# A two-layer transformer program put into one block, its stage barriers replaced by waits on data, and the end of its last expert layer rearranged

## The reference, cut to what matters

```
# first part
h = ada(rms_norm(x));  a = dsa_attention(h);  b = mla_attention(h)
x = x + (sigmoid(gd)*(a @ w_br_dsa) + sigmoid(gm)*(b @ w_br_mla)) @ w_out   # the mix
x = x + memory_cross_attention(rms_norm(x), mem)
x = x + moe(rms_norm(x))              # 16 experts in 4 groups, 2 taken, width 256
# second part, on ctx and x
[ctx, x] += gate * ssd_mixer(rms_norm([ctx, x]))
[ctx, x] += gate * expert_choice(rms_norm([ctx, x]))   # 16 experts of width 1024, each takes 32 rows of a stream
x += gate * attention(rms_norm([ctx, x]))
x += gate * expert_choice(rms_norm(x))
out = rms_norm(x) * final_norm_w
```

## Time and profile before

| | |
|---|---|
| median of three runs | 2198.77 us (2197.3, 2198.77, 2200.84) |
| the profiled execution: its time, its span | 2203.04 us, 2201.2 us |
| mean granted TensorE clock | 0.978 |
| PE, DVE, ACT, POOL busy | 2015.5 us (92%), 941.5 (43%), 648.8 (29%), 106.7 (5%) |
| read from device memory | 620.80 MB, mean 283 GB/s over the span |
| ends of the eight inner blocks | 101.2, 158.1, 213.3, 280.4, 354.1, 585.0, 1070.4, 1721.6 us |

### The profile page before, as it was taken

How to read it: one execution, slowest core, us unless ns; L and a number is a source line. 1 busy time by engine, 2 the same in 40 slices (tenths; PEclk the granted TensorE clock), 3 DMA queues, 4 the chain that set the end, 5 groups by cost and what they waited for, 6 DMA issues and landing times. The chain is left out here.

```text
span 2201.2 us, 24642 instructions
## 1 busy us (share of the span) xinstructions
PE 2015.5 (92%) x9980; PEld 1059.4 (48%) x9980; DVE 941.5 (43%) x1655; ACT 648.8 (29%) x1285; POOL 106.7 (5%) x121
## 2 busy tenths in 40 slices
PE   9987988999899999999899998988999899999887
PEld 6844444444377888878643333322445432222222
DVE  4776224444688878863612221212565310000002
ACT  5244023111277677662221111100235111111000
POOL 0101010000010110010100000000110000000000
PEclk9989998999899999999999999999999999999999
DMA  9537477899333433323589999999830599999996
GB/s 342 194 115 286 172 282 293 338 389 389 112 99 107 143 115 113 118 77 148 216 344 427 427 427 428 428 428 428 327 115 1 231 422 427 425 428 426 425 427 291
DMA packets 142768, 623.58 MB, mean 283 GB/s; under 512 B 10912, under 2 KB 61216, under 8 KB 104512
## 3 DMA queue, kind: packets, MB, share of 16 engines
q1 hardware_dynamic: 138144, 601.92, 68.6%
q0 software_dynamic: 2352, 16.91, 2.0%
q10 hardware_dynamic: 2160, 3.18, 0.4%
HBM read 620.80 MB, written 1.18 MB: 283 GB/s over the span
## 5 line engine op out<-in xcount | busy, mean ns | idle before, releaser
L2901 PE MATMUL bank<-slots,xgTe 128*64 128x512 f32 (+1 forms) x1664 | 373.4, 595 | 34.8 <-DMA slots<-in_moe_w 33.1
L3121 DVE TENSOR_TENSOR actse<-sge,bank 32x512 f32<-32x512 f32 (+1 forms) x48 | 32.8, 683 | 503.6 <-PE bank L2901 281.2
L2901 PEld LDWEIGHTS bank<-slots,xgTe 128*64 128x64 f32 (+1 forms) x1664 | 107.4, 124 | 276.8 <-issue 228.6
L2901 PE MATMUL bank<-slots,aTe 128*64 128x512 f32 (+1 forms) x704 | 161.8, 602 | 13.9 <-issue 13.9
L3019 ACT ACTIVATE sge<-bank 32x512 f32<-32x512 f32 (+1 forms) x48 | 28.4, 591 | 483.6 <-PE bank L2901 483.4
L529 PE MATMUL bank<-slots_r 128*128 128x512 f32 x416 | 164.1, 395 | 0.0
L528 PE MATMUL bank<-hT_r,slots_r 128*128 128x512 f32 x384 | 155.6, 405 | 0.0
L530 PE MATMUL bank<-slots_r 128*128 128x512 f32 x384 | 152.0, 396 | 0.0
L598 PE MATMUL bank<-slots,hT 128*128 128x512 f32 (+1 forms) x320 | 133.2, 578 | 5.3 <-DVE hT L495 3.0
L2125 DVE TENSOR_TENSOR slots_r<-slots,slots_r 128x2048 fp32r<-128x2048 f32 x32 | 76.7, 2397 | 68.2 <-ACT slots_r L2120 68.1
L372 POOL TENSOR_SCALAR rstd<-eps_rows 128x1 f32<-128x1 f32 (+5 forms) x41 | 17.5, 427 | 1768.0 <-ACT xn L445 619.2
(11 more groups left out here) (567 smaller groups left out, 3123.9 us busy)
## 6 DMA issues: line engine op xcount, KB each, us to landing
slots<-in_moe_w SPq DMA_DIRECT2D x148, 2048.0 KB, 29.2
slots<-in_ada_w SPq DMA_DIRECT2D x24, 2048.0 KB, 12.2
extra0e<-in_moe_w SPq DMA_DIRECT2D x23, 2048.0 KB, 27.9
slots<-in_ssd_in_w SPq DMA_DIRECT2D x48, 512.0 KB, 5.3
slots<-in_moe_w_gate SPq DMA_DIRECT2D x23, 1024.0 KB, 10.5
slots<-in_moe_w_up SPq DMA_DIRECT2D x23, 1024.0 KB, 12.6
slots<-in_moe_w_down SPq DMA_DIRECT2D x23, 1024.0 KB, 7.3
rowsB<-acum_rows POOLq DMA_DIRECT2D x16, 1024.0 KB, 5.9
```

What stands on the lines that cost most here:

```text
L2901: i = pe.matmul(bank[64 * n:64 * n + NJ * CAP, :], lhsT(4 * h + k), wv[:, 0, n * 512:(n + 1) * 512], start=(h == 0 and k == 0), stop=(h == ...
L3121: i = dve.tensor_tensor(acts[r_, :], sg[r_, :], psum[1][r_, :], ALU.mult)
```

## The change

1. One block for the whole program: `whole` is opened once, and `block = scope.enter_context(nc.Block())` becomes `block = whole` in all stages. The eight inner ends of blocks are gone; the program's own first and last ones stay.
2. Waits on data where the barrier stood for them. `scalar_squares` gets a condition for each tile: in the memory attention (where the memory tiles now come first), the MoE, the SSD stage and both expert layers. The mix's first matmul on MLA's output waits for that output; the first expert layer's VectorE begins with a wait for the SSD's last add; new semaphores `ssd_added` and a list `att_added` count finished tiles; the extra places of an expert layer count as free with them. The MLA norm and the SSD's y norm move to columns 60 and up of `eps_rows` and `rstd`.
3. In layer 1, both scatters of expert e-1 stand behind expert e's up matmuls, X goes into the sum banks by four matmuls with the identity in front of expert 0's scatter, and the adds to X are gone.
4. In layer 1 the last expert's second up piece (93) is loaded in three parts and its second down piece (95) in two, each with a semaphore of its own, and TensorE waits part by part. `scale` of the last expert signals each 32-row half; the last scatter goes by column half first.
5. The final norm: `fin` is scaled ahead of the last `scale`. ScalarE squares the four sum banks, with a row sum for each; VectorE multiplies each bank by `fin`; GpSimd adds two row sums and takes the root; ScalarE scales output tile 0 and VectorE tile 1, and each is stored by its own semaphore.

```diff
+        whole = ctx.enter_context(nc.Block())
...
-            block = scope.enter_context(nc.Block())
+            block = whole
...
+                            if (t, n, m) == (0, 0, 1):
+                                pe.wait_ge(emptied[DVE], banks["mla", "pv", MLA_H // 2 - 1].done)
...
-            norm = NormT("n2", [X[:, t, :] for t in range(NT)] + [M[:, t, :] for t in range(NT)], xn, hT,
+            norm = NormT("n2", [M[:, t, :] for t in range(NT)] + [X[:, t, :] for t in range(NT)], xn, hT,
+            ready = lambda i: (mem_loaded, 16) if i < NT else (emptied[DVE], banks["mixed", i - NT, 1].done)
...
-                act.wait_ge(mem_loaded, 16)
-                norm.scalar_squares(act)
+                norm.scalar_squares(act, ready)
...
-                norm.scalar_squares(act)
+                norm.scalar_squares(act, lambda t: (emptied[DVE], banks["memo", t, 1].done))
...
-                act.wait_ge(ctx_loaded, 16)
-                norm.scalar_squares(act)
+                norm.scalar_squares(act, lambda t: (ctx_loaded, 16) if t < NT else
+                                    (emptied[DVE], banks["sc1", PAIRS - 1, t - NT, 1].done))
...
-                        dve.tensor_tensor(streams[t][:, c], streams[t][:, c], p_, ALU.add)
+                        i = dve.tensor_tensor(streams[t][:, c], streams[t][:, c], p_, ALU.add)
+                    i.then_inc(ssd_added, 1)
...
-                extra_room[l].freed = (bank_full, len(banks.order))
+                extra_room[l].freed = (ssd_added, TT) if l == 0 else att_added[-1]
...
+                cuts, apart = {6 * N_EXP - 3: ((0, 2, 3, 4), (0, 1)), 6 * N_EXP - 1: ((0, 3, 4), (2,))}.get(n, ((), ()))
+                if cuts:
+                    parts = [(a * D, 1, (b - a) * D, src[:, :, a * D:b * D]) for a, b in zip(cuts, cuts[1:])]
...
+                                if k and k in piece.cuts:
+                                    pe.wait_ge(*piece.apart[piece.cuts.index(k)])
...
+                            if NJ == 1 and e == 0:
+                                pe.matmul(psum[sum_bank(e, t, q)][:, :], ident, X[:, t, n * 512:(n + 1) * 512], start=True,
+                                          stop=False, skip_group_check=True)
...
+                        if e > 0 and l == 1:
+                            scatter(e - 1, 1)
                         pe.wait_ge(a_ready, e + 1)
...
-                               between=(lambda: scatter(e - 1, 1)) if e > 0 else None)
-                    scatter(N_EXP - 1, 0)
-                    scatter(N_EXP - 1, 1)
+                               between=(lambda: scatter(e - 1, 1)) if e > 0 and l == 0 else None)
+                    if l == 1:
+                        scatter_last()
...
-                    norm.scalar_squares(act)
+                    norm.scalar_squares(act, lambda t: (ssd_added, t + 1) if l == 0 else att_added[t])
...
+                        for u, (n, t) in enumerate(LAST):
+                            act.wait_ge(sc_full, u + 1)
+                            act.activation(y[:, t, n * 512:(n + 1) * 512], psum[sum_bank(N_EXP - 1, t, n)][:, :], ACT.Square,
+                                           accum_out=eps_rows[:, NT * n + t:NT * n + t + 1]).then_inc(f_squared, 1)
+                        act.wait_ge(f_weighed, 1)
+                        act.wait_ge(f_rooted, 1)
+                        act.activation(y[:, 0, :], y[:, 0, :], ACT.Copy, scale=rstd[:, 0:1]).then_inc(f_done[0], 1)
...
+                    if l == 0:
+                        dve.wait_ge(ssd_added, TT)
                     link(dve.memset(wide, 0.0))
...
+                            i = dve.tensor_tensor(y[:, t, c], psum[sum_bank(N_EXP - 1, t, n)][:, :], fin[:, c], ALU.mult)
...
+                        dve.wait_ge(f_rooted, NT)
+                        dve.tensor_scalar(y[:, 1, :], y[:, 1, :], rstd[:, 1:2], None, ALU.mult).then_inc(f_done[1], 1)
```

More of the change, by code:

```diff
@@ L241, in build, with weights @@
         stream = []
-        def weights(name, parts, slot=None):
+        def weights(name, parts, slot=None, apart=()):
             if slot is None:
                 slot = 0 if not stream else (stream[-1][2] + 1) % SLOTS
-            piece = ring.add(name, slot, len(parts))
+            piece = ring.add(name, slot, len(parts) - len(apart))
+            if apart:
+                piece.apart = [(piece.sem, piece.full)]
+                for j in apart:
+                    half_total[j] += 16
+                    piece.apart.append((half_loaded[j], half_total[j]))
             stream.append((piece, parts, slot))
@@ L339, in moe2_weights @@
                     parts = [(0, 1, SLOT, src)]
-                weights(("moe2", l, n), parts, where)
+                weights(("moe2", l, n), parts, where, apart)
+                if cuts:
+                    stream[-1][0].cuts = cuts
         moe2_weights(0, (5, 4, 3, 0, 1, 2, SLOTS))
@@ L362, in load_weights @@
                     sp.wait_ge(*piece.before.freed)
-                for at, k, n, src in parts:
-                    sp.dma_start(view(piece, at, k, n), src).then_inc(piece.sem, 16)
+                for m, (at, k, n, src) in enumerate(parts):
+                    landed = piece.sem if piece.apart is None else piece.apart[m][0]
+                    sp.dma_start(view(piece, at, k, n), src).then_inc(landed, 16)
                 issued[0] += 1
```

114 lines of the change are left out of this document (67 added, 47 removed).

## The result

The changed kernel takes 2184.22 us (median of 4 runs, 2178.59 to 2185.93), against 2198.03 for the kernel before in the same set: 13.8 us less, where 19.3 was forecast. The ratio is given as 0.9931, with an interval of 0.991 to 0.9951, which is a gain of 10.8 to 19.8 us. The time lies 4.7 us above the forecast and inside the range. A second set of five runs gave 2182.42 us and a ratio of 0.9921 (0.9908 to 0.9934), a gain of about 17. The profiled execution of the changed kernel took 2185.93 us, with a span of 2183.9 us and a mean clock of 0.982, so the two profiled executions are 17.3 us apart in span, nearer to the forecast than the two medians. The mean clocks of single executions run from 0.976 to 0.983 for the kernel before and from 0.981 to 0.987 for the change.

What follows compares the result with a forecast made beforehand. TensorE's order of work was taken as the bound up to the SSD stage's end, the weight-piece stream in both expert layers; 15.05 (boundaries) + 1.9 + 2.4 = 19.35 us off 2198.77 gave 2179.5 us, range 2175 to 2189.

Steps and rivals of the forecast that it cites:

- Boundary 4: Mix to memory attention: TensorE's idle 1.62 us and its 1.08 us stall on `ada_buf` go, gain 2.5 us.
- Boundary 5: Memory attention to MoE: squares run before the last add, the 1.29 us gap and TensorE's stall go, gain 3.1 us.
- Boundaries 6, 7 and 8: MoE to SSD, SSD to first expert layer, attention to second: last scalings end sooner, gains 2.4, 2.8 and 2.1 us.
- The identity matmuls: Second expert of the second expert layer: 3.7 us more on TensorE, priced at 0 because the DMA stream hides it.
- Rival (b): Head of the second expert layer: TensorE is the bound, identity matmuls cost their whole 3.7 us; 2183 us, chance 0.17.
- The last expert: End of the second expert layer: pieces in parts and the moved scatter gain 1.9 us, bounds 0.5 to 2.5.
- The tail: From the last expert's output through the final norm to the stores: 2.4 us gained, bounds 1.0 to 3.2.
- (a): Stage boundaries give only their bare gaps, as some wait holds the early squares; 2190 us, chance 0.23.
- (c): More gain than counted, as more stalls of the `ada_buf` kind go; 2174 us, chance 0.06.
- (d): Stages up to 1070 us: TensorE's clock falls without its rests at the boundaries; about 2206 us, chance 0.03.
- The rule on batching: Last pieces: batching transfers to 1 MiB or more would make the parts 2 us slower, the total gain 17.4.
- (e): Every boundary remains as a wait in an in-order queue, only the kernel's end gains 4.3 us; 2194.5 us, chance 0.04.

Runs made afterwards that it cites:

- dummies: The changed kernel with dummy matmuls added in TensorE's gaps at the head of the first expert layer; ratio 0.9912 to the kernel before.
- the control: The changed kernel run once more, nothing altered, in a second set of five runs: median 2182.42 us, ratio 0.9921 to the kernel before.

## Why the prediction came out as it did

**The boundaries, step by step.** Read at the place itself, each last scaling or stall came about as much sooner as forecast. Boundary 4: from the last add to TensorE's first transposes, 289.10 - 279.74 = 9.36 us before and 280.05 - 273.49 = 6.56 now, 2.8 for a forecast of 2.5. (The 0.1 allowed there for a queue fetch shows in no row: TensorE goes on without a gap.) Boundary 5: the squares follow the add by 0.03 us in place of 1.29, the stall of 2.04 is gone, and the modulation's first transposes start 2.89 us behind the add in place of 6.15, 3.3 for 3.1 (the row of 2.10 us is one square, not a pair); the cover of the router's weights, priced at 0 to 2, was too thin by 0.7 us in this trace, so at the router's matmuls 2.6 is left. Boundaries 6, 7 and 8: 2.42, 2.89 and 1.88 for 2.4, 2.8 and 2.1. The first freed piece of the second layer came 14.93 us sooner for 15.05.

**Boundaries 5 and 6 together** arrived only in part: 2.8 of 5.5 us. From the router's matmuls to the MoE's last add the change took 219.24 us for 218.38 (the other kernels 218.40 to 222.06), and the cause of that spread is open. At boundary 6 the last scaling ends 2.42 us sooner, but TensorE's first matmul behind its transposes starts at 9.42 us behind the add in place of 10.45, and the SSD's last add comes 1.08 sooner. The clock is low here too (a mean of 0.66 over the 10 us behind the add, 0.54 before), and the transposes take 5.79 us (6.39 before). It looks like boundary 7's pattern, but it wasn't tried by an experiment.

**Where that step failed in spite of its sum**: "A microsecond won before either layer moves its start, and with it its first freed place, one for one". At boundary 7 it didn't; 0.04 of 2.89 us arrived in this trace (39.30 to 39.26), and 0.85 in the mean: the nine profiles that have neither a barrier there nor dummies take 38.56, the three with the barrier 39.41. The prediction priced the transposes as queueing (2.8 in place of 3.1) and didn't read the clock, 0.50, at which they run. The sum came out right because other stretches gained more than forecast: the one to the mix's add 6.25 us for 2.15, and the one from the first layer's freed piece to the attention's add, where the code is the same, 1.29 for nothing. Over the twelve kernels with equal code the first stretch gains anything from 1.5 to 6.3 us on the kernel before. That part was luck of the execution, not insight.

**The identity matmuls** are the term that was wrong: "I take 0", with about 1 us to spare. It cost 2.1 us, for two reasons. The price on TensorE was 6.5 us and not 3.7, since the scatter matmuls between them slow down too. And in expert 0 the clock was at 0.66 and 0.68 over the 5 us with the down matmuls, in the trace before and in the changed one, which takes from the lead. In kernels whose clock stayed at 1.00 there, the stretch took 437.11 us with the identity matmuls in expert 0 (all barriers back) and 435.78 or 436.08 with them in expert 10, so the cost was 1.0 to 1.3. Rival (b), 3.7 passed on whole, was half true: TensorE's time does pass on to the stream, but only what exceeds a lead of some 4.4 us. The prediction's sign for this, TensorE idling on DMA anew early in the layer, didn't show (no such wait from 1730 to 1900 us): the stream lost its 2 us unseen there, and they came out at the layer's end.

**The last expert**: 1.9 was forecast, and from its third piece to its last gate scaling it gained 2.2 (19.76 to 17.56): parts 1.4, scatter 0.9, by the two kernels that lack one of them. (The wait of 1.21 us in the prediction's rows stands before the fourth piece, not the third.) Against it the third piece starts 1.6 us later after the first freed one, 421.38 for 419.75, which is the hole's doing (419.32 with the identity matmuls moved); so the stretch shows 438.94 for 439.51. It was sized well, and the 0.6 of the table is no measure of it.

**The tail**: 1.80 (12.53 to 10.73) for 2.4, well inside the bounds of 1.0 to 3.2. The squares of a bank took 0.60 as estimated. Two terms were small: the last scaling ends at 2180.08, which is 7.0 us behind the last matmul (2169.43 + 3.63) for a forecast of 6.75, since both roots go through GpSimd in turn; and behind it the stores, which leave together, take 3.8 us where one store took 3.0 (2196.92 + 1.28 to 2201.2), and only 0.45 had been set off for that.

**The sum against the medians.** 15.05 + 1.9 + 2.4 = 19.35 was forecast; the traces give 14.9 + 0.6 + 1.8 = 17.3. The rest of the way to 13.8 is in the choice of executions: the kernel before was profiled in an execution of 2203.04 us, 5.0 over the 2198.03 of this set, the change in one that is 1.7 over its own. A difference of two medians of four runs, each with runs 4 to 7 us apart, is uncertain by 4.5 us either way (0.991 to 0.9951), and the control's interval is 14.5 to 20.2 us. So neither set of runs excludes the 19.3 of the forecast; that some of its terms were wrong is known from the traces alone.

**The rivals.** (a), bare gaps only, falls: every chain started earlier. (c) didn't happen. (d), slower through the clock: the mean clock rose, 0.978 to 0.982, with the gaps gone, so its sign was wrong for the whole; on a small scale it happened at boundary 7, and perhaps at 6. The Trainium skill, TensorE: Matmul & The Clock Gate, Part 1, says that idleness brings the low clock back. The rows agree for the transposes (0.50 behind idle times of 5.3 and 3.4 us); that the same pair of waits of 1.0 and 1.3 us is followed by a full clock in one kernel and by half in the other also fits its remark that the monitor runs on its own time and not on the kernel's. The rule on batching in the Trainium skill, DMA: Bandwidth & Descriptors, section Bandwidth, would have cost 2 us for the pieces in parts. The parts gained 1.4 us in the last expert, and the third piece started at most 0.4 us later with them than without (421.31 to 421.51 for 421.09, from the first freed piece), so here the measurement decides against applying it to transfers that stand in a full queue. (e) is excluded by the kernel with all barriers, which loses the gain that (e) says was never there.

## What to carry to other kernels

Where stages meet, look for work of the next stage whose inputs are long ready, and for the engine that stands in its queue before it: at boundaries 5 to 8 the barrier's own gap was 0.3 to 1.3 us of the 1.9 to 3.3 won at the place; at boundary 4 it was 1.6 of 2.8. Then look for what TensorE must do behind that chain, and at what clock: a last scaling that ends 2.9 us sooner left 1.75 behind the transposes at boundary 7, since they had become the bound. Work that is moved into a stretch where a stream of transfers lives on freed places is not free because the engine has time on average; count the lead that the freed places have at that point, with the worst clock seen there, and put such work where the engine waits for data anyway. To price a change in one expert, read it in that expert, from one piece's start to the output: over the whole stretch the moved scatter read 0.2 us, and in the last expert 0.9. When a few us are in question, compare stretches between shared marks in several profiles as well as medians: the stretches with no clock dip in them repeated to 0.1 us (10.72 to 10.77 for the end), while the four medians of the kernel before, from sets on more than one chip, lie between 2198.03 and 2202.78.

## What was not expected of the hardware

Gains at single places did not add up here, and TensorE's clock is why at boundary 7. The same code with the same two waits ran its gather in 7.41 or 9.03 us, and which of them came depended on what lay before, not on the waits: with the barrier at boundary 7 it was 7.41 in all three profiles, without barrier and dummies 8.9 to 9.0 in eight of nine. Equal code from the start to the mix took 273.49 to 278.27 us in the twelve kernels without barriers there. The 2.9 us won at boundary 7 arrived as anything from 0.0 to 2.8 us (39.27 to 36.46 for 39.30).
